# Turning the first group's rows beside two units of a bridge instead of one, in a two-layer diffusion backbone on one Trainium2 core

## The chip, the cores and the metric

The kernel runs on one core of one Trainium2 chip. The metric is the time of one execution on the device in microseconds (us); lower is better. A core has five engines that run their own instruction streams and meet at semaphores: PE (TensorE, matmuls and transposes), DVE (VectorE), ACT (ScalarE), POOL (GpSimd) and SP (SyncE, here only a queue that issues DMAs).

## The reference, cut to what matters

Two post-norm layers work on 512 latent tokens of 1024 channels and, in the first layer, on 256 context tokens beside them. Each layer is a token mixer (grouped-query attention, neighbourhood attention and Fourier mixing, merged by gates) followed by a SwiGLU channel mixer. The change touches the place where the mixer ends and the channel mixer begins:

```
y = _merge(gz, oa, ob, oc, w_branch, w_out)          # ends with  y @ w_out
x = _layernorm(DEEPNORM_ALPHA * x + g1 * y, ln1_g[l], ln1_b[l])
f = _swiglu(_modulate(_layernorm(x), sh2, sc2), w_gu[l], w_down[l])
```

So between two products (with `w_out` and with `w_gu`) there are two layer norms over the channels of a token, and a modulation by per-channel scale and shift.

## The kernel before, in words

Weights stream from memory in units of 1024 columns of 128 rows (512 KB), in two halves. SP loads a unit into `raw` (two slots), ACT copies it to `w_hi` (L797), POOL makes the remainder `w_lo` (L719), and PE takes three products per tile of the contraction (`w_lo` by `x_hi`, `w_hi` by `x_lo`, `w_hi` by `x_hi`; L2320 for a group of columns), so that fp32 accuracy comes out of a faster format. A unit of these stages is 8 steps k of 3 matmuls, 24 in all. SP may load unit u only when POOL has finished unit u-2, and ACT splits unit u+2 when PE has finished unit u.

Activations lie with channels on partitions (`acc`, `h_hi`, `h_lo`: 8 tiles of 128 channels by up to 768 tokens), but a layer norm needs tokens on partitions. A phase called `bridge` does the change-over. There are two per layer: the first, `part` 0, which the code calls `lead`, stands between `w_out` and the gate and up products; the second, `part` 1, between the down product and the next layer. A bridge splits the tokens into two groups so that the norm of one group runs beside the products of the other. For the first bridge the groups are 3 and 3 tiles of 128 tokens in layer 0 (384 columns) and 2 and 2 in layer 1 (256 columns).

PE's order in a first bridge, for group g and unit n:

1. 8 units of the first group with `w_out`; then 8 units of the second group with the same weights. After the second group's unit 0, `turn_rows` transposes the first group's `acc` to tokens on partitions (L2376).
2. `turn_columns` (L2361) transposes the normed rows `xn` back, one channel tile k at a time: it waits for `xn` of all tiles of the group at k = 0, and for `h_lo` of channel tile k-4 from k = 4 on (four PSUM banks in turn). It is called through `between`, a function that `group_columns` calls after the three matmuls of each step k. Before the change all eight calls lie in the second group's unit 7, one after each step.
3. The first gate unit of the first group (the "lead unit" below), whose step k waits for `h_lo` of channel tile k; then `turn_rows` of the second group, and so on.

ACT's order beside it, in `norm_work(0, n)` after each unit n of the second group: ACT first waits for unit n, splits unit n+2 and evacuates unit n to `acc` (L1242, `produced`), and then does a part of the norm: squares at n = 0, 2 and 3 in layer 0, `applied` at n = 5, which writes the first and, of three tiles, the third tile of `xn` (L854; DVE writes the other, L1561), and at n = 6 the DMAs that store `xr` (L867) and `modulated` for all eight channel tiles. `modulated` waits for the turned tile k, applies scale and shift in PSUM (L878), and for odd k copies it to `h_hi` (L884). DVE makes `h_hi` for even k (L1575) and `h_lo` for every k (L1569, `parts_of_h`).

Of the kernel before, what the change touches and what calls it, by code (L numbers as in the profile page):

```python
# [16 lines left out]
KD = D // P  # L17
# [159 lines left out]
def late_chunks(ph):  # L177

    return LATE if ph.kind == "bridge" and ph.layer == 0 and ph.part == 1 else 0
# [44 lines left out]
def slot_of(ph, g, i):  # L224

    return 3 * g + i if len(ph.groups[0]) < 4 else ph.groups[g][i]
# [22 lines left out]
def ends(ph):  # L249

    return ph.layer == DEPTH - 1 and ph.part == 1
# [61 lines left out]
def build(nc, x_in, ctx_in, cond, cond_cols, w_first, w_ada, b_ada, stream, qk_gain, norm_rows, bias, ident_in,  # L313
# [177 lines left out]
    def S(name):  # L491
        if name not in sems:
            sems[name] = nc.alloc_semaphore(name)
        return sems[name]
# [14 lines left out]
    def at(ph, name):  # L509

        return ph.at.get(name, 0) + (PRIME if name in PRIMED else 0)
# [60 lines left out]
    with block:  # L572
# [208 lines left out]
        def _(act):  # L781
# [54 lines left out]
            def squares(ph, g, second, some=slice(None)):  # L836

                tiles, of = ph.groups[g], xn_first if ph.kind == "first_norm" else xn
                base = (2 - ends(ph)) * len(ph.groups[0]) * g + second * len(tiles) * (ph.kind == "bridge")
                for i, t in list(enumerate(tiles))[some]:  # L840

                    act.wait_ge(S("mean_ready"), at(ph, "mean_ready") + base + i + 1)
                    if second and ph.kind == "bridge":
                        act.wait_ge(S("shifted"), at(ph, "shifted") + len(ph.groups[0]) * g + i + 1)
                    nc.scalar.activation(of[:, slot_of(ph, g, i), :], row_tile(ph, g, i, second), ACT.Square, bias=neg_mean[:, second, t:t + 1],
                                         accum_out=square_s[:, second, t:t + 1]).then_inc(S("squared"), 1)

            def applied(ph, g):

                tiles, of = ph.groups[g], xn_first if ph.kind == "first_norm" else xn  # L850
                act.wait_ge(S("root_ready"), at(ph, "root_ready") + (2 * g + 2 if ph.kind == "bridge" else 1))
                for i in range(0, len(tiles), 2):
                    t = tiles[i]
                    nc.scalar.activation(of[:, slot_of(ph, g, i), :], xr[:, t, :], ACT.Identity,  # L854
                                         scale=inv_s[:, ALLT + t:ALLT + t + 1],
                                         bias=shift_s[:, t:t + 1]).then_inc(S("normed"), 1)

            def store(ph, g):
                for i, t in enumerate(ph.groups[g]):
                    act.wait_ge(S("shifted"), at(ph, "shifted") + len(ph.groups[0]) * g + i + 1)  # L860
                    dst = out[t, :, :] if ends(ph) else scratch[2 * ph.layer + ph.part + 1, t, :, :]
                    if last_rows(ph, g) and i == len(ph.groups[g]) - 1:
                        act.dma_start(out[t, :, 0:LAT], xr[:, t, 0:LAT]).then_inc(S("stored"), 16)
                        act.wait_ge(S("shifted"), at(ph, "shifted") + len(ph.groups[0]) * g + i + 2)
                        act.dma_start(out[t, :, LAT:D], xr[:, t, LAT:D]).then_inc(S("stored"), 16)
                        continue
                    act.dma_start(dst, xr[:, t, :]).then_inc(S("stored"), 16)  # L867

            def modulated(ph, g, k):

                layer, part, m = modulated_into(ph)
                a, b = columns_of(ph.groups[g])
                if k == 0:
                    act.wait_ge(S("mods_ready"), MODS_READY[layer, part])
                act.wait_ge(S("turned"), at(ph, "turned") + KD * g + k + 1)
                for x, y, c in by_condition(a, b):
                    some = turned_columns(ph, k, x - a, y - a)
                    last = nc.scalar.activation(some, some, ACT.Identity,  # L878
                                                scale=mods_v[:, layer, m + 1, k, c:c + 1],
                                                bias=mods_v[:, layer, m, k, c:c + 1])  # L880
                last.then_inc(S("h_val"), 1)
                if k % 2:
                    act.wait_ge(S("h_val"), at(ph, "h_val") + KD * g + k + 1)
                    nc.scalar.activation(h_hi[:, k, a:b], turned_columns(ph, k, 0, b - a), ACT.Copy).then_inc(S("h_hi_odd"), 1)  # L884
# [349 lines left out]
            def bridge(ph):  # L1234
# [37 lines left out]
                def norm_work(g, n):  # L1272

                    tiles = len(ph.groups[g])
                    steps = {4: ((4, 0, 1), (5, 1, 2), (6, 2, 4)), 3: ((2, 0, 1), (3, 1, 3)),
                             2: ((3, 0, 1), (4, 1, 2)) if g and lead else ((3, 0, 2),)}[tiles]
                    if n == 0:
                        squares(ph, g, 0)
                    for step, first, end in steps:
                        if n == step:  # L1280
                            squares(ph, g, 1, slice(first, end))
                    if n == (6 if tiles > 3 else 5):
                        applied(ph, g)
                    if n == 6:
                        store(ph, g)
                        for j in range(KD):
                            modulated(ph, g, j)

                if lead:
# [974 lines left out]
        def _(pe):  # L2264
# [86 lines left out]
            def turn_columns(ph, g):  # L2351

                def between(k):
                    if k == 0:
                        even = len(ph.groups[0]) - len(ph.groups[0]) // 2
                        pe.wait_ge(S("normed"), at(ph, "normed") + even * g + (len(ph.groups[g]) + 1) // 2)
                        pe.wait_ge(S("normed_odd"), at(ph, "normed_odd") + len(ph.groups[0]) // 2 * g + len(ph.groups[g]) // 2)
                    if k >= 4:
                        pe.wait_ge(S("h_lo"), at(ph, "h_lo") + KD * g + k - 3)
                    for i in range(len(ph.groups[g])):  # L2360
                        last = nc.tensor.transpose(ps[:, TURNED_BANK[k % 4], i * P:(i + 1) * P],  # L2361
                                                   xn[:, slot_of(ph, g, i), k * P:(k + 1) * P], ident[:, :])
                    last.then_inc(S("turned"), 1)
                return between
# [431 lines left out]
            def bridge(ph):  # L2796
# [28 lines left out]
                def produced(g, n, between=lambda k: None):  # L2825

                    a, b = columns_of(ph.groups[g])
                    m = pass_unit(ph, g, n)
                    emptied(m)
                    group_columns(ph.unit + m, n % 2, m % PRODUCT_BANKS, x_hi, x_lo, k_tiles, a, b,  # L2830
                                  late_ready if g and late_chunks(ph) else ready, between
                                  ).then_inc(S("unit_done"), 1)
# [10 lines left out]
                turn = turn_columns(ph, 0)  # L2843
                for n in range(KD):
                    between = lambda k: None
                    if late_chunks(ph):
                        if n - 1 in LATE_TURNS:
                            between = lambda k: turn(LATE_TURNS[n - 1][k // 3]) if k % 3 == 1 and k // 3 < len(LATE_TURNS[n - 1]) else None
                    elif n == KD - 1 and not ends(ph):
                        between = turn  # L2850
                    produced(1, n, between)
                    if n == 0 and not late_chunks(ph):
                        turn_rows(ph, 0)
# [14 lines left out]
                for g, tiles in enumerate(ph.groups):  # L2868
                    a, b = columns_of(tiles)
                    for c in range(LEAD):  # L2870
                        u, n = first + 2 * LEAD * g + 2 * c, LEAD * g + c
# [10 lines left out]
                        else:  # L2882
                            pe.wait_ge(S("silu"), at(ph, "silu") + n)
                        group_columns(u + 1, 1, lead_bank(g, 2 * c + 1), h_hi, h_lo, KD, a, b,
                                      between=turn_columns(ph, 1) if g == 0 and c == LEAD - 1 else lambda k: None
# [68 lines left out]
            for ph in phases:  # L2954
                work = {"first_norm": first_norm, "modulate": modulate, "fourier_in": fourier_in, "tokens_a": tokens_a,
                        "fourier": fourier, "merge_c": merge_c, "merge_a": merge_a, "merge_b": merge_b, "values": values,
                        "attention": attention, "bridge": bridge, "gate_up": gate_up, "down": down}.get(ph.kind)
                if work:
                    work(ph)
# [350 lines left out]
```

## Time and profile before

| | |
|---|---|
| median of 3 runs | 2280.64 us (2278.1 to 2283.69) |
| profiled execution, its own time | 2281.39 us |
| its span in the trace | 2279.5 us |
| PE matmul busy | 2225.3 us (98%) |
| DVE, ACT, POOL busy | 1251.2, 970.6, 1140.8 us |
| mean granted TensorE clock | 0.996 |
| layer 0's first bridge | about 716 to 863 us of the span |
| layer 1's first bridge | about 1841 to 1955 us |

The span counts from the first to the last instruction of the trace; the own time adds what lies around it, 1.9 us. A timeline row gives start, duration, engine, line, operation and tiles; in square brackets stands the idle time of the engine before it and who ended it. PE rows overlap, since matmuls are pipelined: the distance of two starts tells the cost, not the duration of one.

### The profile page before, as it was taken

Reading aid. Unit: us, or ns where it says so; the run is one execution under the profiler, and the core shown is the slowest. Engines: PE = TensorE matmul, PEld = TensorE weight load, DVE = VectorE, ACT = ScalarE, POOL = GpSimd, SP = SyncE. Lnnn points to the kernel's source line nnn. Section 1 sums busy time; section 2 is a strip of 40 time slices with the busy share of each in tenths; the row PEclk is TensorE's granted clock in tenths of the full one; section 3 lists DMA queues with packets and bytes.
Section 4 is the critical chain, followed back from the end, with each engine's and each line's share of the span. In section 5 each row is a group of like instructions: output and inputs, shape, how many; then the busy total and the mean of one; then the engine's idle time right before and its main releaser. Section 6 shows DMA issues by size and latency. Waiting matters only on the chain.

```text
span 2279.5 us, 34252 instructions
## 1 busy us (share of the span) xinstructions
PE 2225.3 (98%) x12866; PEld 2034.6 (89%) x12866; DVE 1251.2 (55%) x2515; ACT 970.6 (43%) x1918; POOL 1140.8 (50%) x898
## 2 busy tenths in 40 slices
PE   7999999999999999999999999999999999999997
PEld 4899989999999999999998888888889899888887
DVE  5979766538732555875351456866548535412114
ACT  4232366537632652133232363366447456222223
POOL 1333445435634554456464653555545577544545
PEclk9999999999999999999999999999999999999999
DMA  6534300122214546412224463511223265533335
GB/s 272 213 119 130 105 26 29 47 86 75 73 56 134 169 136 208 153 61 77 78 87 138 144 225 134 194 48 37 86 83 97 85 197 185 203 94 105 110 118 184
DMA packets 122973, 273.50 MB, mean 120 GB/s; under 512 B 14020, under 2 KB 14276, under 8 KB 121032
## 3 DMA queue, kind: packets, MB, share of 16 engines
q1 hardware_dynamic: 112464, 245.42, 33.1%
q10 hardware_dynamic: 10360, 26.09, 3.4%
q8 instruction: 93, 1.52, 0.3%
q14 instruction: 56, 0.46, 0.1%
HBM read 257.82 MB, written 10.49 MB: 118 GB/s over the span
## 4 chain that ended last, share of the span: by engine, by line
PE 84%; DVE 7%; ACT 4%; DMA 2%; POOL 2%; issue 1%; ACTq 1%; SPq 0%; DVEq 0%
PE ps L2308 29%; PE ps L2320 13%; PE ps L2310 9%; PE ps L2737 8%; PE ps L2421 7%; PE ps L2915 6%; PE ps L2690 3%; PE ps L2672 3%; PE ps L2653 3%; DMA raw<-in_stream 1%; PE ps L2497 1%; POOL w_lo L719 1%; DVE pt L1911 1%; DVE max_c L1894 1%; ACT p_sb L1109 1%
## 5 line engine op out<-in xcount | busy, mean ns | idle before, releaser
L719 POOL TENSOR_TENSOR w_lo<-raw,w_hi 128x512 fp32r<-128x512 f32 x608 | 825.4, 1379 | 805.2 <-ACT w_hi L797 799.4
L797 ACT ACTIVATE w_hi<-raw 128x512 fp32r<-128x512 f32 x600 | 349.7, 627 | 567.6 <-PE ps L2308 173.5
L731 POOL TENSOR_TENSOR p_sb<-p_sb,row_inv 128x768 f32<-128x768 f32 (+1 forms) x160 | 178.9, 1126 | 195.8 <-DVE row_inv L1904 194.4
L2308 PE MATMUL ps<-h_hi,w_lo 128*128 128x512 f32 (+1 forms) x672 | 251.2, 374 | 1.1 <-POOL w_lo L719 1.1
L2308 PE MATMUL ps<-h_lo,w_hi 128*128 128x512 f32 (+1 forms) x672 | 250.5, 373 | 0.0
L2308 PE MATMUL ps<-h_hi,w_hi 128*128 128x512 f32 (+1 forms) x672 | 250.5, 373 | 0.0
L2021 DVE TENSOR_TENSOR ps<-silu_g,ps 128x512 f32<-128x512 f32 (+3 forms) x52 | 36.7, 706 | 248.4 <-PE ps L2308 172.7
L2737 PE MATMUL ps<-h_hi,w_lo 128*128 128x384 f32 (+1 forms) x408 | 146.8, 360 | 0.7 <-ACT gates_a L1146 0.7
L2737 PE MATMUL ps<-h_lo,w_hi 128*128 128x384 f32 (+1 forms) x408 | 144.2, 353 | 0.0
L2737 PE MATMUL ps<-h_hi,w_hi 128*128 128x384 f32 (+1 forms) x408 | 144.0, 353 | 0.0
L2308 PEld LDWEIGHTS ps<-h_hi,w_lo 128*128 128x128 f32 x672 | 126.2, 188 | 19.8 <-POOL w_lo L719 1.5
L2308 PEld LDWEIGHTS ps<-h_hi,w_hi 128*128 128x128 f32 x672 | 126.2, 188 | 18.3
L2308 PEld LDWEIGHTS ps<-h_lo,w_hi 128*128 128x128 f32 x672 | 126.2, 188 | 18.2
L1109 ACT ACTIVATE p_sb<-ps,neg_max 128x768 f32<-128x768 f32 (+1 forms) x160 | 117.0, 731 | 49.2 <-DVE neg_max L1891 39.6
L1911 DVE TENSOR_TENSOR pt<-ps,pt 128x512 fp32r<-128x512 f32 x176 | 118.3, 688 | 22.2 <-ACT pt L1117 20.5
L1117 ACT ACTIVATE pt<-ps 128x512 fp32r<-128x512 f32 x176 | 101.7, 598 | 57.5 <-PE ps L2672 56.6
L2320 PE MATMUL ps<-h_hi,w_lo 128*128 128x256 f32 (+2 forms) x352 | 112.2, 319 | 3.2 <-POOL w_lo L719 2.2
L2320 PE MATMUL ps<-h_lo,w_hi 128*128 128x256 f32 (+2 forms) x352 | 109.6, 311 | 0.0
L2320 PE MATMUL ps<-h_hi,w_hi 128*128 128x256 f32 (+2 forms) x352 | 109.6, 311 | 0.0
L2033 DVE SCALAR_TENSOR_TENSOR acc<-ps,mods,acc 128x256 f32<-128x256 f32 (+4 forms) x64 | 33.6, 548 | 123.7 <-PE ps L2320 64.5
L2672 PE MATMUL ps<-ident,p_sb 128*128 128x128 f32 x704 | 96.7, 275 | 2.8 <-POOL p_sb L731 1.3
L2421 PE MATMUL ps<-w_lo,h_hi 128*128 128x512 f32 (+1 forms) x272 | 96.9, 356 | 0.3 <-ACT u_cols L924 0.3
(283 smaller groups left out, 5901.8 us busy)
## 6 DMA issues: line engine op xcount, KB each, us to landing
raw<-in_stream SPq DMA_DIRECT2D x648, 256.0 KB, 3.0
ada_raw_gate_up<-in_w_ada SPq DMA_DIRECT2D x30, 512.0 KB, 4.1
ada_raw_tokens_a<-in_w_ada SPq DMA_DIRECT2D x25, 512.0 KB, 5.6
ada_raw_merge_c<-in_w_ada SPq DMA_DIRECT2D x25, 512.0 KB, 4.5
bias_sb<-in_bias ACTq DMA_DIRECT2D x32, 256.0 KB, 2.8
scratch<-xr ACTq DMA_DIRECT2D x16, 512.0 KB, 5.0
xr<-scratch SPq DMA_DIRECT2D x14, 512.0 KB, 5.3
first_raw<-in_w_first SPq DMA_DIRECT2D x5, 1024.0 KB, 14.1
```

What stands on the lines that cost most here:

```text
L719: nc.gpsimd.tensor_tensor(w_lo[:, u % 2, cols], raw[:, u % 2, cols], w_hi[:, u % 2, cols].bitcast(F32), ALU.subtract).then_inc(S("lo_made" ...
L731: nc.gpsimd.tensor_tensor(p, p, row_inv[:, c:c + 1].broadcast_to([P, keys]), ALU.mult).then_inc(S("p_ready"), 1)
L797: nc.scalar.activation(w_hi[:, s, cols], raw[:, s, cols], ACT.Copy).then_inc(S("hi_made"), 1)
L1109: nc.scalar.activation(p_sb[branch][n % 2][i][:, 0:keys], region(branch, i, 0, keys), ACT.Exp, bias=neg_max[:, i:i + 1], accum_out=row_sum ...
L1911: nc.vector.tensor_tensor(pt_lo[branch][:, a:a + w], ps[:, turn_bank(ph, order), 0:w], pt_hi[branch][:, a:a + w].bitcast(F32), ALU.subtrac ...
L2308: last = nc.tensor.matmul(bank(0), tile, x[:, k, 0:split], start=start, stop=stop)
L2310: last = nc.tensor.matmul(bank(1), tile, x[:, k, HALF:TOK], start=start, stop=stop)
L2320: last = nc.tensor.matmul(ps[:, bank, 0:b - a], w[:, s, k * P:(k + 1) * P], x[:, k, a:b], start=k == 0 and name == TERMS[0], stop=k == k_t ...
L2421: last = nc.tensor.matmul(ps[:, banks[t], 0:cols], x[:, k, t * P:(t + 1) * P], w[:, s, kk * cols:(kk + 1) * cols], start=k == 0 and name = ...
L2672: last = nc.tensor.transpose(ps[:, turn_bank(ph, order), col:col + P], p_sb[branch][n % 2][i][:, a:a + P], ident[:, :])
L2737: last = nc.tensor.matmul(ps[:, bank, 0:b - a], w[:, u % 2, k * P:(k + 1) * P], x[:, k, a:b], start=r == 0, stop=r == FILL_STEPS - 1, skip ...
L2915: last = nc.tensor.matmul(ps[:, bank, 0:HALF], half_slot(w, slot)[:, k * P:(k + 1) * P], x[:, first + k, a:a + HALF], start=FACTOR_BEGINS[ ...
```

## The change

PE calls `turn` for the first group's channel tiles 0 to 3 in the second group's unit 6 and for tiles 4 to 7 in unit 7, each after an odd step k, in place of all eight in unit 7. ACT modulates tiles 0 to 3 directly after `applied`, at n = 5 and so before it waits for unit 6, and tiles 4 to 7 at n = 6. The number of instructions stays the same. The condition leaves out the second bridge of both layers (`late_chunks` in layer 0, `ends` in layer 1), so that the first bridge of either layer is changed and nothing else; `norm_work` with g = 1 keeps its order.

```
@@ ACT, norm_work(g, n)
                     if n == (6 if tiles > 3 else 5):
                         applied(ph, g)
+                        if g == 0:
+                            for j in range(KD // 2):
+                                modulated(ph, g, j)
                     if n == 6:
                         store(ph, g)
-                        for j in range(KD):
+                        for j in range(KD // 2 * (g == 0), KD):
                             modulated(ph, g, j)
@@ PE, bridge(ph)
-                    elif n == KD - 1 and not ends(ph):
-                        between = turn
+                    elif n >= KD - 2 and not ends(ph):
+                        between = lambda k, n=n: turn((n - KD + 2) * KD // 2 + k // 2) if k % 2 else None
                     produced(1, n, between)
```

## Rows read from the trace of the kernel before

**Rows 1.** The page, parts 1 and 2: busy shares, and the granted clock by slice.

```profile
PE 2225.3 (98%) x12866; PEld 2034.6 (89%) x12866; DVE 1251.2 (55%) x2515; ACT 970.6 (43%) x1918; POOL 1140.8 (50%) x898
...
PEclk9999999999999999999999999999999999999999
```

**Rows 2.** The chain that ended last, a turn in each layer: start, us, what.

```profile
781.79 0.33 PE ps L2361 x3
...
1888.05 0.22 PE ps L2361 x2
```

**Rows 3.** Timeline of PE in layer 0, units 6 and 7 and the lead unit.

```profile
776.95 0.33 PE L2320 MATMUL ps<-y_hi,w_lo 128*128 128x384 f32 x1
...
777.82 0.33 PE L2320 MATMUL ps<-y_hi,w_hi 128*128 128x384 f32 x1
...
781.11 0.33 PE L2320 MATMUL ps<-y_hi,w_lo 128*128 128x384 f32 x1
...
781.63 0.49 PE L2361 MATMUL ps<-ident,xn 128*128 128x128 f32 x3
...
787.93 0.42 PE L2320 MATMUL ps<-h_hi,w_lo 128*128 128x384 f32 x1
```

**Rows 4.** Timeline of ACT in layer 0, from unit 5's end on.

```profile
777.15 1.15 ACT L797 ACTIVATE w_hi<-raw 128x512 fp32r<-128x512 f32 x2 [2.39 <-PE ps L2320]
...
778.82 2.37 ACT L854 ACTIVATE xn<-xr,shift_s,inv_s 128x1024 f32<-128x1024 f32 x2
...
783.18 1.21 ACT L878 ACTIVATE ps<-ps,mods 128x384 f32<-128x384 f32 x2
784.41 0.49 ACT L884 ACTIVATE h_hi<-ps 128x384 fp32r<-128x384 f32 x1
```

**Rows 5.** Timeline of PE in layer 1, units 6 and 7 and the lead unit.

```profile
1879.95 0.35 PE L2320 MATMUL ps<-y_hi,w_lo 128*128 128x256 f32 x1 [0.65 <-ACT acc L1242]
...
1880.62 0.28 PE L2320 MATMUL ps<-y_hi,w_hi 128*128 128x256 f32 x1
...
1882.91 0.36 PE L2320 MATMUL ps<-y_hi,w_lo 128*128 128x256 f32 x1
...
1887.25 0.44 PE L2361 MATMUL ps<-ident,xn 128*128 128x128 f32 x2 [1.45 <-DVE h_lo L1569]
...
1889.32 0.36 PE L2320 MATMUL ps<-h_hi,w_lo 128*128 128x256 f32 x1
```

**Rows 6.** Timeline of ACT in layer 1, the same stretch.

```profile
1880.82 1.25 ACT L854 ACTIVATE xn<-xr,shift_s,inv_s 128x1024 f32<-128x1024 f32 x1
1883.09 0.63 ACT L797 ACTIVATE w_hi<-raw 128x512 fp32r<-128x512 f32 x1 [1.03 <-PE ps L2320]
1884.81 0.63 ACT L797 ACTIVATE w_hi<-raw 128x512 fp32r<-128x512 f32 x1 [1.09 <-DMA raw<-in_stream]
...
1885.74 0.99 ACT L878 ACTIVATE ps<-ps,mods 128x256 f32<-128x256 f32 x2
```

**Rows 7.** Timeline of POOL in layer 1, the same stretch.

```profile
1878.57 6.72 POOL L719 TENSOR_TENSOR w_lo<-raw,w_hi 128x512 fp32r<-128x512 f32 x5 [1.73 <-ACT w_hi L797]
1885.52 1.26 POOL L719 TENSOR_TENSOR w_lo<-raw,w_hi 128x512 fp32r<-128x512 f32 x1 [0.23 <-ACT w_hi L797]
```

**Rows 8.** Loads of `raw` between 1878 and 1898 us, issue to landing.

```profile
DMA to landing us min/median/max: 2.6/3.6/5.4
```

**Rows 9.** Windows: us, busy (count) of PE, PEld, DVE, ACT, POOL, granted clock, DMA share, GB/s.

```profile
15.00:20.00 5.00, 0.52 (x4) 0.16 (x3) 3.65 (x6) 4.92 (x10) 0.00 (x0) 1.00 1.02 408
20.00:24.00 4.00, 4.00 (x13) 1.21 (x12) 3.63 (x10) 1.55 (x4) 2.52 (x2) 0.57 1.04 413
25.00:27.30 2.30, 0.35 (x5) 0.26 (x4) 2.30 (x4) 2.30 (x4) 0.00 (x0) 0.94 0.98 403
27.30:29.20 1.90, 1.79 (x8) 1.43 (x8) 0.79 (x6) 1.26 (x3) 1.32 (x2) 0.50 1.05 420
...
1885.50:1887.50 2.00, 0.55 (x6) 0.35 (x4) 1.16 (x3) 1.97 (x6) 1.26 (x1) 1.00 0.97 322
```

## The prediction, made before the changed kernel ran

> **What bounds the kernel now.** I read the page first: PE is busy for 98% of the span at a clock whose every slice is at full speed [rows 1]. So time moves only when PE's stream of matmuls gains or loses a gap. Then I read the chain of work that ended last in both first bridges: the turns lie on it as PE work, one of three transposes costing 0.33 us in layer 0 and one of two costing 0.22 us in layer 1 [rows 2]. The timelines of PE and ACT give the clock times of units 6 and 7, the timeline of POOL and the loads tell what a later split would do to the weights, and the windows show what the granted clock did after PE had stood idle.
>
> In layer 0, unit 6 starts at 776.95, unit 7 at 781.11, so a bare unit costs 4.16 us, 0.52 a step [rows 3]. Unit 7 with its eight turns lasts to the lead unit at 787.93: 6.82 us, and the work alone is 4.16 + 8 x 0.33 = 6.80. The turns wait for practically nothing there. ACT modulates two tiles and copies one in 783.18 to about 784.8, some 1.6 us a pair [rows 4], while PE offers a pair every 2 x (0.52 + 0.33) = 1.7 us. The two just fit.
>
> In layer 1 they don't. Unit 7 runs from 1882.91 to the lead unit at 1889.32, 6.41 us [rows 5]. Its work is 24 matmuls at 0.12 (from 1879.95 to 1880.62 five steps, the first a little longer, so 2.88) + 8 x 0.22 = 4.64. So 1.77 us are waits, 1.45 of them in one gap before the turn of tile 4, for `h_lo` of tile 0 [rows 5]. Behind it stands ACT: it could not modulate tile 0 before 1885.74, since it first waited 1.03 us for unit 6 and 1.09 us for a late half of `raw` [rows 6].
>
> **The change part by part.**
>
> *Instructions.* None is added. The turns, 8 calls per bridge, keep their 0.33 and 0.22 us each on PE, ACT's and DVE's rows their durations. The sum has only waits.
>
> *The wait for `xn` in layer 0.* The turn of tile 0 needs all rows of `xn`. ACT writes its two tiles of them at n = 5 from 778.82 to 778.82 + 2.37 = 781.19 [rows 4]; nothing in the change brings that forward, since ACT is ordered behind unit 5 (its split starts at 777.15). Before, the turn came at 781.63, 0.44 us after. Now it stands after step 1 of unit 6. The last of those six matmuls starts at 777.82 [rows 3], so PE would go on at 777.82 + 0.17 = 777.99. It stands until 781.19: a stall of 3.20 us. PE works in order: the other 18 matmuls of unit 6, which have no need of `xn`, are queued behind the turn, and unit 7 behind them. From there unit 6 ends at 781.19 + 4 x 0.33 + 6 x 0.52 = 785.63, unit 7 at 785.63 + 4.16 + 4 x 0.33 = 791.11, against 787.93 before: +3.2 us. Bounds: a stall is at least 3.1 (if PE's wait ends a little into the row's modelled end), and with a restart penalty like the 0.42 instead of 0.34 us that a first matmul shows, at most 3.4.
>
> *What is late next in layer 0.* ACT is now inside `modulated` until tile 3 is turned at 785.6 and done, 785.6 + 0.25 + 0.6 + 0.5 = 787.0; only then it splits the lead unit's weights (1.15 us, which it did from unit 6's end at 781.2 before) and POOL follows (1.3 us a half, as five of them in 6.72 us in layer 1 [rows 7]): first half at about 788.9, second at 790.2. PE wants them at 791.1 and 793.2. Hidden, with 2 us to spare. If that cover were gone the cost would be what exceeds 2 us. The modulation of tiles 4 to 7 takes ACT from 788.7 to 792.0 and the lead unit's step 7 is at 794.8: hidden as well. DVE is idle but for these. Term: 0, and between 0 and 0.5.
>
> *Layer 1.* The stall comes here too: the six matmuls of steps 0 and 1 end at 1880.62 + 0.12 = 1880.74, ACT's row of `xn` at 1880.82 + 1.25 = 1882.07 [rows 5, 6]. Loss 1.33 us. Against that the 1.77 us of waits in unit 7 go: tile 0 can be modulated at about 1882.6 in place of 1885.74, ahead of the wait for unit 6 and for the late half of `raw`, and the turn of tile 4 now comes about 3.5 us after that of tile 0 plus ACT's lead. New end of unit 7: 1882.07 + 6 x 0.36 + 4 x 0.22 = 1885.11, and + 2.88 + 0.88 = 1888.87, against 1889.32: -0.45 us. Taken: -0.5 with the gap's own restart (0.44 in place of 0.38) gone. Bounds: 0, if one of the new lags below eats it, and -1.8, if the stall for `xn` were not there.
>
> *What is late next in layer 1.* ACT splits the lead unit's two halves at about 1886.3 and 1886.9 instead of 1883.09 and 1884.81. POOL, which had finished them at 1878.57 + 6.72 = 1885.29 and 1886.78 [rows 7], finishes at about 1888.3 and 1889.6. PE wants them at 1888.9 and 1890.3: covered by 0.6 us. SP's queue is behind POOL: the loads of two units later leave 3.0 and 2.8 us later, and land 2.6 to 5.4 us after issue [rows 8], so at 1891 to 1893.7 and 1892.2 to 1895. ACT asks for them after the lead unit, at 1892.4, and PE at about 1896.4. The latest landing leaves POOL's first half done in time (1893.7 + 0.6 + 1.3 = 1895.6), and delays ACT's next work, squares of the second group, due at 1895.3, by 0.4 at most. The two stores on ACT's queue move from the end of that split to about 1887.8 and now share the DMA engines with these loads; that is in the 5.4. Term: 0, at most +0.5.
>
> Sum: +3.2 - 0.5 = +2.7 us, bounds 3.1 - 1.8 = +1.3 and 3.4 + 0.5 + 0.5 = +4.4. After the bridges everything hangs on PE's order, so the shift is carried to the end. Against the profiled execution: span 2282.2, own time 2281.39 + 2.7 = 2284.1. That execution lay 0.75 us over the median of 2280.64, so the median should be 2283.3, +0.12%. A measurement of this kernel tells about 0.3%, 6.8 us, from no change; the three runs shown lie 5.6 us apart.
>
> **The clock.** PE's new gap of 3.2 us in layer 0 is longer than any in the bridges now. What rows show: in 15 to 20 us PE did 0.52 us of work, and in 20 to 24 the clock was 0.57 of full; in 25 to 27.3 it did 0.35, and in 27.3 to 29.2 the clock was 0.50, the lower level of 1.2 GHz. After the 1.45 us gap in layer 1, in which 2 us held 0.55 us of busy time, it stayed at 1.00 [rows 9]. So 1.45 us in dense work is survived, and 2 us amid the sparse work of the start is not; 3.2 us lies between dense units and is open. The price if it falls: half of the time at 1.2 GHz. The fall after 20 us covers 0.57 x 4 us, so (1 - 0.57) x 4 x 2 = 3.4 us at half speed, which costs 1.7; one twice as long costs 3.4. The Trainium skill ("TensorE: Matmul & The Clock Gate", "Why this matters for your kernels") tells to leave no long idle gaps between bursts of matmuls, lest the clock go back to half; by that rule the new gap speaks for rival 2 and its time, and without it the sum stands. The trace agrees as far as its starting stretch goes.
>
> **The rivals.**
>
> 1. *The stall is given back.* PE's gap in layer 0 is absorbed by a wait later in the same bridge, and only layer 1's gain is left: -0.5, 2280.1 us. For it: PE has small waits after the lead unit. Against it: all of them are released by engines that PE itself releases, so they shift with it. 7%.
> 2. *The clock falls* after the gap of layer 0 and PE works at half speed for 3.4 to 6.8 us: +2.7 + 1.7 to 3.4 = +4.4 to +6.1, 2285.0 to 2286.7 us. Still within 0.3%. 15%.
> 3. *Slower, on the other side.* The same fall, but lasting: PE loses half of each microsecond at the lower level, so beyond 2 x (6.8 - 2.7) = 8.2 us at half speed the sum passes 6.8. At 10 us the price is 5, the time 2288.3. For it: nothing but that no row shows how dense work recovers here; against it: both falls at the start ended within 7 us. 4%.
> 4. *The change does what its order suggests*, and is faster: layer 0's turn does not wait for `xn` because ACT has it early, and layer 1 keeps its full 1.8 us: -1.8, 2278.8. Against it stands ACT's row [rows 4], ordered behind unit 5. It is not over 0.3% either. 2%.
>
> **How the numbers follow.** The forecast has the remaining 72%. Faster by over 0.3% would want 6.8 us of gain, and the first bridges have not 2 us of waits at this place: 0.01, for a measurement that errs. Slower: rival 3, and the upper end of rival 2 with a measurement that adds a microsecond: 0.06. Same: 0.93. The range takes the bounds +1.3 to +4.4, the spread of a median of three from runs 5.6 us apart (about 1.5 to either side), and reaches to most of rival 2 above: 2280.0 to 2287.5.
>
> **What would show it.** In layer 0 PE's row of the first turn (L2361) carries an idle time of 3.2 us, released by ACT L854, in the middle of unit 6, and the lead unit starts 3.2 us later than before. In layer 1 the same row has 1.3 us, and the gap of 1.45 us for `h_lo` is gone; the lead unit starts some 0.5 us earlier relative to unit 6. ACT's split of the lead unit comes after the modulation of tile 3, and no PE row waits for POOL there. The granted clock is 1.00 in the windows after 781 us. The prediction is wrong if that clock is 0.5 for several us, if `xn` comes earlier than 781.2, or if in layer 1 the loads of `raw` come so late that ACT and then PE stand after the lead unit.

## The result, and the profile after

The changed kernel takes 2285.74 us in the median of 8 runs (2281.65 to 2287.13), the kernel before 2281.23 us in 8 runs beside it (2277.79 to 2285.17). The ratio is 1.0018 with a 95% interval of [1.001, 1.0027]: +4.1 us, or between +2.3 and +6.2. A second series of the same kernel gave 1.002 [1.0011, 1.0029]. The predicted time of 2283.3 us is 2.4 us short of it. The range of 2280.0 to 2287.5 us held it, and the change is under 0.3%, as foreseen.

The page of the changed kernel, parts 1 and 2:

```profile
PE 2226.8 (97%) x12866; PEld 2037.6 (89%) x12866; DVE 1249.6 (55%) x2515; ACT 971.3 (43%) x1918; POOL 1144.3 (50%) x898
...
PEclk9999999999999999999999999999999999999999
```

The number of instructions is that of [rows 1], and slices of 57 us are too coarse to show anything. One has to go to the two bridges. The profiled execution took 2287.03 us, span 2285.1. Absolute times differ between executions by up to 4 us before the changed code begins, so I measure distances, called stretches below: from the first group's `turn_rows` (the first row of `ident,acc`) to the lead unit's first matmul (`h_hi,w_lo`). First the kernel before, PE's timeline, `turn_rows` in layer 0 and in layer 1:

```profile
752.76 1.91 PE L2376 MATMUL ps<-ident,acc 128*128 128x128 f32 x16
...
1862.47 1.91 PE L2376 MATMUL ps<-ident,acc 128*128 128x128 f32 x16
```

The changed kernel, PE's timeline:

```profile
749.91 1.91 PE L2379 MATMUL ps<-ident,acc 128*128 128x128 f32 x16
...
778.38 0.90 PE L2364 MATMUL ps<-ident,xn 128*128 128x128 f32 x3 [3.07 <-ACT xn L854]
...
780.04 0.52 PE L2323 MATMUL ps<-y_hi,w_lo 128*128 128x384 f32 x1
780.36 0.52 PE L2323 MATMUL ps<-y_lo,w_hi 128*128 128x384 f32 x1
...
791.13 0.42 PE L2323 MATMUL ps<-h_hi,w_lo 128*128 128x384 f32 x1
...
1866.62 1.91 PE L2379 MATMUL ps<-ident,acc 128*128 128x128 f32 x16
...
1886.19 0.44 PE L2364 MATMUL ps<-ident,xn 128*128 128x128 f32 x2 [1.25 <-ACT xn L854]
...
1894.47 0.36 PE L2323 MATMUL ps<-h_hi,w_lo 128*128 128x256 f32 x1
```

In layer 0 the stretch was 787.93 - 752.76 = 35.17 us (its end is in [rows 3]) and is 791.13 - 749.91 = 41.22: +6.05. The first turn waits 3.07 us for ACT's rows of `xn`, as foreseen. But the matmuls behind it start 0.32 us apart, and not 0.17 as in the kernel before. In layer 1 it was 1889.32 - 1862.47 = 26.85 [rows 5] and is 1894.47 - 1866.62 = 27.85: +1.00, where -0.45 was foreseen. The 1.45 us wait for `h_lo` [rows 5] is gone, and one of 1.25 us for `xn` has come. The windows of the changed kernel tell the rest; columns as in [rows 9], the granted clock is the third number from the end:

```profile
774.00:778.00 4.00, 1.30 (x8) 0.98 (x6) 0.00 (x0) 3.70 (x6) 2.49 (x2) 0.94 0.40 129
778.00:782.00 4.00, 3.62 (x14) 3.53 (x15) 1.11 (x2) 1.09 (x3) 0.00 (x0) 0.50 0.24 84
782.00:786.00 4.00, 4.00 (x21) 3.87 (x19) 1.41 (x3) 1.81 (x4) 0.00 (x0) 0.71 0.00 0
786.00:790.00 4.00, 4.00 (x28) 3.90 (x28) 1.54 (x4) 3.94 (x9) 2.39 (x2) 1.00 0.64 251
...
1885.00:1887.00 2.00, 0.81 (x6) 0.81 (x7) 0.69 (x1) 1.41 (x3) 2.00 (x3) 0.95 0.57 183
1887.00:1890.00 3.00, 3.00 (x16) 3.00 (x15) 1.27 (x3) 1.37 (x4) 1.06 (x1) 0.50 0.61 187
1890.00:1893.00 3.00, 3.00 (x26) 3.00 (x26) 1.27 (x3) 2.31 (x6) 0.43 (x1) 0.96 0.26 103
```

After the gap in layer 0 the clock stood at its lower level, 1.2 GHz. Adding (1 - clock) x length over the first three windows and doubling gives 2 x (0.24 + 2.0 + 1.16) = 6.8 us at half speed, which costs 3.4 us of PE's work less what of it fell into the gap itself. In layer 1 it is 2 x (0.1 + 1.5 + 0.12) = 3.4 us. So two things are to be told apart by experiments: the gap's own length and the clock after it.

ACT's timeline of the changed kernel in layer 0, against [rows 4]:

```profile
775.96 2.36 ACT L854 ACTIVATE xn<-xr,shift_s,inv_s 128x1024 f32<-128x1024 f32 x2
779.38 0.64 ACT L878 ACTIVATE ps<-ps,mods 128x384 f32<-128x384 f32 x1 [1.05 <-PE ps L2364]
...
786.91 0.62 ACT L797 ACTIVATE w_hi<-raw 128x512 fp32r<-128x512 f32 x1
```

ACT splits the lead unit's weights at 786.91, after the modulation of tile 3, in the order that the prediction laid out. POOL's two rows behind it start at 787.61 and take 2.54 us, so the first half was ready at about 788.9, 2 us ahead of the lead unit's start, and no PE row of the stretch waits for POOL. In layer 1 POOL's first half was ready 0.6 us ahead (1893.84 against 1894.47), as the prediction had it.

### The profile page after: what moved, and what is told of

Its sections match the earlier page's. It is cut to its first block, busy times and chain, and to the rows that moved or that the text cites. A ratio compares the mean times of both kernels' runs of the same rounds, so it can differ in the third digit from the quotient of the medians.

```text
span 2285.1 us, 34252 instructions
## 1 busy us (share of the span) xinstructions
PE 2226.8 (97%) x12866; PEld 2037.6 (89%) x12866; DVE 1249.6 (55%) x2515; ACT 971.3 (43%) x1918; POOL 1144.3 (50%) x898
## 4 chain that ended last, share of the span: by engine, by line
PE 85%; DVE 7%; ACT 4%; POOL 2%; DMA 1%; issue 1%; ACTq 1%; SPq 0%; DVEq 0%
PE ps L2311 29%; PE ps L2323 14%; PE ps L2313 9%; PE ps L2740 8%; PE ps L2424 7%; PE ps L2918 6%; PE ps L2693 3%; PE ps L2675 3%; PE ps L2656 2%; PE ps L2500 1%; DMA raw<-in_stream 1%; POOL w_lo L719 1%; DVE pt L1914 1%; DVE max_c L1897 1%; ACT p_sb L1109 1%
```

## The experiments

All variants set two tables, one entry per layer: which turn stands after which step, and how many tiles ACT modulates ahead of unit 6's wait. "Before" is eight turns in unit 7 and none ahead, "changed" the turns after odd steps of units 6 and 7 and four ahead.

```
+LEAD_TURNS = (turns of layer 0, turns of layer 1)   # {(unit, step): tile}
+TURNED_AHEAD = (ahead in layer 0, ahead in layer 1)
+APPLIED_AT = (5, 5)                                 # after which unit ACT writes its rows of xn
+EXTRA = (0, 0)                                      # extra matmuls ahead of the first turn
```

The cuts of code below give what differs from the changed kernel; "before" and "changed" stand for the whole table.

The stretches below are from the one profiled execution of each run, as above; the ratio comes from the medians of some ten executions and is to the kernel before on the same chip. The profiled execution need not be a typical one: that of the run with layer 1 alone was the slowest of its eleven, those with layer 0 alone and with early rows the fastest of nine and of eleven. Where the table has "one execution", no ratio was measured.

In layer 0 the four traces with the old order there agree to 0.03 us. In layer 1 the five with the old order there (before, layer 0 only, rows early, and the two kernels with the first turn at step 3 and at step 5) give 26.33 to 26.85, mean 26.58, so that half a microsecond says little there.

| run | layer 0: first turn waits, us at half clock, stretch | layer 1: the same | ratio, interval |
|---|---|---|---|
| before | 0, 0, 35.17 | 0 (1.45 for `h_lo`), 0, 26.85 | |
| changed | 3.07, 6.8, 41.22 | 1.25, 3.4, 27.85 | 1.0018 [1.001, 1.0027] |
| changed, 2nd | 3.07, 0, 38.47 | 1.55, 3.4, 27.86 | 1.002 [1.0011, 1.0029] |
| changed, 3rd | 3.07, 3.4, 39.76 | 1.34, 0, 26.45 | one execution |
| gap filled | 0, 0, 38.49 | 0, 0, 26.32 | 1.0022 [1.0013, 1.0031] |
| gap filled, 2nd | 0, 0, 38.50 | 1.47, 0, 27.78 | 1.0011 [1.0002, 1.002] |
| layer 0 only | 3.07, 3.4, 39.90 | as before, 0, 26.79 | 1.0027 [1.0017, 1.0037] |
| layer 1 only | as before, 0, 35.20 | 1.41, 3.4, 27.83 | 1.0 [0.9991, 1.0009] |
| rows early | 0, 0, 35.40 | as before, 0, 26.57 | 1.0002 [0.9993, 1.0011] |
| first turn at step 3 | 2.03, 3.4, 38.94 | as before, 0, 26.37 | one execution |
| first turn at step 5 | 1.00, 0, 36.39 | as before, 0, 26.33 | one execution |
| late turns in layer 1 | as before, 0, 35.18 | 0, 0, 25.25 | 0.9994 [0.9985, 1.0003] |
| the same, 2nd | as before, 0, 35.20 | 0, 0, 25.31 | 0.9993 [0.9984, 1.0002] |
| rows early, late turns | 0, 0, 35.40 | 0, 0, 25.21 | 0.9999 [0.999, 1.0009] |

**The gap filled.** The changed kernel with busy matmuls in place of the idle time.

```
+EXTRA = (18, 11)
...
+    for _ in range(EXTRA[ph.layer]):          # the bank of unit 7, which starts it anew
+        nc.tensor.matmul(ps[:, (pass_unit(ph, 1, n) + 1) % PRODUCT_BANKS, 0:b - a],
+                         w_hi[:, n % 2, k * P:(k + 1) * P], x_hi[:, k, a:b], start=True, stop=True)
```

> The changed kernel with 18 extra matmuls of 384 columns (layer 0) and 11 of 256 (layer 1) on PE between step 1 of unit 6 and the first turn, into a PSUM bank that nobody reads: the gap's time stays, its idleness goes. Theory A (the gap for xn costs its length, and the idle gap also lets the clock fall): the first turn waits under 0.3 us, the clock stays at 1.00 in both bridges, the lead unit comes 3.2 us later than before in layer 0, and the time is +2.7 us on the kernel before (ratio 1.0012), so some 1.5 to 4 us under the changed kernel. Theory B (the excess over +2.7 us is weights or loads that come late, not the clock): the time stays that of the changed kernel, ratio 1.0018 to 1.0025.

PE's timeline of this kernel in layer 0, the first turn and the lead unit (`turn_rows` began at 751.27):

```profile
779.74 0.55 PE L2369 MATMUL ps<-ident,xn 128*128 128x128 f32 x3
...
789.76 0.42 PE L2328 MATMUL ps<-h_hi,w_lo 128*128 128x384 f32 x1
```

and its windows:

```profile
774.00:778.00 4.00, 4.00 (x25) 4.00 (x24) 1.22 (x3) 2.34 (x5) 2.38 (x3) 1.00 0.42 131
778.00:782.00 4.00, 4.00 (x26) 3.68 (x25) 0.90 (x2) 2.62 (x4) 0.90 (x1) 1.00 0.41 131
```

The turn waits for nothing and the clock holds 1.00. The stretch is 38.49: +3.32, the 3.07 us of the gap and some 0.2 more. In layer 1 it is 26.32, between the -0.45 foreseen and no change, as far as the spread there tells. So the excess of the changed kernel, 2.7 us in layer 0 and 1.5 in layer 1, is not there once PE has work in the gap: Theory A, in the trace. The time was less clear. 1.0022 is above the 1.0012 that these +2.8 us would give, so I ran it again beside the changed kernel. The expectation for the filled kernel comes first, that for the changed one second.

> The kernel with the extra matmuls in the gaps once more. Theory A: clock 1.00 at both gaps, +3.3 us in layer 0 and -0.5 in layer 1, ratio 1.0012, 3 to 4 us under the changed kernel on this chip. Theory B (the extra over +2.7 us is not the clock): the same time as the changed kernel.

> The changed kernel once more, beside the one with the filled gap on the same chip. Theory A (a fall of the clock follows the gap in every execution, 3.4 or 6.8 us long): the stretch to the lead unit of layer 0 is 39.9 or 41.2 us again, that of layer 1 27.8, and the time is +5.7 to +7.1 us, ratio 1.0025 to 1.0031. Theory C (it falls in some executions only, in layer 1 above all): a stretch of 38.4 or 26.4 us turns up, and the ratio stays near 1.0018.

On one chip the changed kernel took 2284.48 us and the filled one 2282.24, ratios 1.002 and 1.0011. The difference of 2.2 us has the sign and size of the clock's share, but the intervals overlap, and in the first series the filled kernel had the higher ratio of the two (1.0022 against 1.0018): the time alone does not settle it. In the second trace of the filled kernel layer 0 is as in the first, 38.50 us at a clock of 1.00. In layer 1 the stretch is 27.78, and not for the clock, which held 1.00 there too: ACT's rows of `xn` came late, since the second half of a unit of `raw` had kept ACT waiting 1.38 us before them, and the turn waited 1.47 us in spite of the extra matmuls:

```profile
1883.12 0.63 ACT L801 ACTIVATE w_hi<-raw 128x512 fp32r<-128x512 f32 x1 [1.38 <-DMA raw<-in_stream]
1883.66 0.46 ACT L1246 ACTIVATE acc<-ps,mods 128x256 f32<-128x256 f32 x1
1884.01 1.23 ACT L858 ACTIVATE xn<-xr,shift_s,inv_s 128x1024 f32<-128x1024 f32 x1
```

The second trace of the changed kernel brought in layer 0 what Theory C had said: the same gap of 3.07 us, and no fall of the clock. Its timeline and its windows:

```profile
778.29 0.55 PE L2364 MATMUL ps<-ident,xn 128*128 128x128 f32 x3 [3.07 <-ACT xn L854]
```

```profile
775.00:779.00 4.00, 0.93 (x7) 0.71 (x6) 0.00 (x0) 3.30 (x6) 2.41 (x2) 1.00 0.45 149
779.00:783.00 4.00, 4.00 (x29) 3.90 (x27) 2.32 (x5) 2.36 (x4) 0.00 (x0) 1.00 0.09 31
```

> The changed kernel a third time, one look, for what the clock does after the gaps. Theory A: 3.4 or 6.8 us at half clock in layer 0 and 3.4 in layer 1, stretches of 39.9 or 41.2 and of 27.8 us. Theory C: the clock stays at 1.00 in one of them.

The third trace has 3.4 us at half speed in layer 0 and none in layer 1. The stretch of layer 0 in the three traces is 41.22, 38.47 and 39.76: with the time at half clock of 6.8, 0 and 3.4 us, some 1.3 to 1.4 us for each 3.4. It is one and the same program with one and the same gap, so this shows the clock's price without any change of code. Theory A as it stood ("in every execution") fell, and Theory C holds. It also weakens one reading of the filled kernel: two traces with the clock at 1.00 do not by themselves show that the extra matmuls kept it there, when one of four without them (the fourth is layer 0 alone, below) held it as well.

**What the stretches leave out.** Some 64 to 67 us behind the start of layer 1's lead unit, at the bridge's end, PE waits once more, for POOL's `w_lo` of weights whose loads reached ACT late. In the second trace of the changed kernel:

```profile
1954.87 2.58 ACT L797 ACTIVATE w_hi<-raw 128x512 fp32r<-128x512 f32 x4 [5.31 <-DMA raw<-in_stream]
...
1956.90 0.50 PE L2311 MATMUL ps<-h_hi,w_lo 128*128 128x512 f32 x1 [2.62 <-POOL w_lo L719]
```

```profile
1954.30:1956.90 2.60, 0.00 (x1) 0.01 (x1) 2.46 (x6) 1.92 (x4) 1.32 (x2) 1.00 0.82 265
1956.90:1961.00 4.10, 4.10 (x11) 3.27 (x12) 3.64 (x5) 0.55 (x1) 4.10 (x3) 0.58 0.96 344
```

The wait is 1.07 us in the kernel before, 1.79, 2.62 and 1.05 in the three traces of the changed one, 2.53 with layer 1 alone changed, 2.73 and 0.22 in the two of the filled one, and from none to 1.06 in the other seven. Behind the two of 2.62 and 2.53 us the clock fell for 3.4 us more, behind the one of 2.73 it did not. The mean is 2.0 us in the four traces with layer 1 changed and its gap unfilled, and 0.6 in the five with the old order there. That points to the change, but no run isolates it, and the measured time of layer 1 alone shows no loss (1.0); whether the change lengthens this wait stays open.

**One layer at a time.** In layer 0 first, then in layer 1.

```
LEAD_TURNS = (changed, before); TURNED_AHEAD = (4, 0)      # layer 0 only
LEAD_TURNS = (before, changed); TURNED_AHEAD = (0, 4)      # layer 1 only
```

> Only layer 0's first bridge turns over two units, layer 1's as before. Theory A: the gap of 3.1 us in layer 0 stays, 6.8 us at half clock follow it in the profile and cost about 2.9, together +3.2 to +6.1 us, ratio 1.0014 to 1.0027. Theory B (both layers carry about the same part of the measured +4.1): +2 us, ratio 1.0009.

> Only layer 1's first bridge turns over two units. Theory A: a gap of 1.25 us for xn and none of 1.45 us for h_lo: -0.45 us when the clock stays, +1.1 us when 3.4 us run at half clock, ratio 0.9998 to 1.0005. Theory B: +2 us, ratio 1.0009.

Layer 0 alone carries the loss: 1.0027, stretch +4.73 with 3.4 us at half clock. Layer 1 alone cannot be told from nothing: its ratio is 1.0. Its stretch is 27.83, 1.25 over the mean of the old order, with 3.4 us at half clock, in an execution that took 2284.18 us where the median was 2278.61. Theory B, half of the loss in each and so 1.0009, is out for layer 0, whose lower bound is 1.0017, and lies at the edge of the interval for layer 1.

**ACT's rows of `xn` one unit earlier**, which takes the gap's cause away.

```
LEAD_TURNS = (changed, before); TURNED_AHEAD = (4, 0)
-APPLIED_AT = (5, 5)
+APPLIED_AT = (4, 5)
```

> As layer 0 only, but ACT writes its rows of xn one unit earlier, after unit 4 and not after unit 5, which their root allows (shift_s was ready at 775.7 us in the trace of before, 3.1 us before ACT took it up). Theory A (the gap is ACT's place in the order, not the norm's length): the first turn of layer 0 waits 0 to 0.2 us, the clock stays at 1.00, and the time is that of the kernel before, ratio 0.9995 to 1.0005. Rival: ACT, waiting for the root, splits unit 7's weights too late and PE stands at unit 7 instead, or the turns beside two units cost PE more than beside one; then 1 to 3 us stay, ratio 1.0005 to 1.0014.

ACT's timeline and the first turn in this kernel:

```profile
772.88 2.38 ACT L858 ACTIVATE xn<-xr,shift_s,inv_s 128x1024 f32<-128x1024 f32 x2 [0.96 <-DVE shift_s L1485]
...
775.31 0.55 PE L2369 MATMUL ps<-ident,xn 128*128 128x128 f32 x3
```

Now ACT waits 0.96 us for the root of the norm, and PE waits not at all. The stretch is 35.40, +0.23, with the turns beside two units; the ratio 1.0002. So the loss of layer 0 was ACT's place in the order and what followed, and the spread turns by themselves cost 0.2 us. The rival, a late split of unit 7's weights, didn't come.

**A ladder of gaps in layer 0**: the first turn after step 3 and after step 5 of unit 6.

```
{(6,3):0, (6,5):1, (6,7):2, (7,1):3, (7,3):4, (7,5):5, (7,6):6, (7,7):7}    ahead 3
{(6,5):0, (6,7):1, (7,1):2, (7,2):3, (7,3):4, (7,5):5, (7,6):6, (7,7):7}    ahead 2
```

> Layer 0 only, the first turn after step 3 of unit 6 and not after step 1: two steps of 0.52 us fewer in the gap. Theory A: the turn waits 2.0 us, and the stretch to the lead unit grows by 2.1 us, plus 1.7 or 3.4 us if the clock falls. Rival (the clock falls only after a gap as long as 3.1 us): +2.1 us and the clock at 1.00.

> Layer 0 only, the first turn after step 5 of unit 6. Theory A: it waits 1.0 us, the stretch to the lead unit grows by 1.1 us, and the clock stays at 1.00, as it did after the 1.45 us gap of layer 1 before. Rival (a gap of 1 us is enough, as after 1.25 us in the changed kernel's layer 1): half clock for 3.4 us and +2.8 us.

The first turn and the windows around it, for step 3 and then for step 5:

```profile
781.00 0.60 PE L2369 MATMUL ps<-ident,xn 128*128 128x128 f32 x3 [2.03 <-ACT xn L858]
```

```profile
778.90:781.00 2.10, 0.07 (x1) 0.00 (x1) 0.00 (x0) 2.05 (x2) 1.24 (x2) 1.00 0.36 124
781.00:783.00 2.00, 2.00 (x9) 2.00 (x10) 0.59 (x2) 0.64 (x1) 0.00 (x0) 0.59 0.43 132
783.00:787.00 4.00, 4.00 (x23) 3.83 (x23) 1.49 (x3) 2.22 (x4) 0.00 (x0) 0.78 0.03 10
```

```profile
778.75 0.55 PE L2369 MATMUL ps<-ident,xn 128*128 128x128 f32 x3 [1.00 <-ACT xn L858]
```

```profile
777.00:779.00 2.00, 1.00 (x7) 0.68 (x6) 0.00 (x0) 1.70 (x2) 0.91 (x1) 1.00 0.44 139
779.00:781.00 2.00, 2.00 (x15) 1.96 (x14) 0.89 (x2) 0.92 (x2) 0.00 (x0) 1.00 0.34 123
```

A gap of 2.03 us was followed by 3.4 us at half speed (2 x (0.82 + 0.88)), stretch +3.77; one of 1.00 us by none, stretch +1.22. The gap's own price is its length, and 0.2 us for the turns' place, in each of the two; what the clock adds comes on top. Each has one trace, so these two do not show how often the clock falls.

**A placement that shortens layer 1's stretch.**

```
layer 1: {(6,5):0, (6,7):1, (7,0):2, (7,1):3, (7,3):4, (7,4):5, (7,6):6, (7,7):7}    ahead 4
```

> Layer 0 as before; in layer 1 the turns of tiles 0 and 1 stand after steps 5 and 7 of unit 6, those of 2 to 7 after steps 0, 1, 3, 4, 6, 7 of unit 7, and ACT modulates tiles 0 to 3 ahead of unit 6's wait. Theory A (the move is good where xn is ready and bad where it is not): the first turn waits under 0.3 us, the 1.45 us wait for h_lo is gone, the clock stays at 1.00, and from turn_rows of the first group to the lead unit it takes 25.1 us in place of 26.85; time -1.7 us, ratio 0.9992, hardly to be told from 1. Rival: the later split of the lead unit's weights takes the wait's place, and the stretch stays above 26.5 us.

> The kernel with layer 0 as before and late turns in layer 1 once more, to tell its gain of 1.6 us in the trace from none: ratio 0.9993 and, with the run before this one, an interval that should lie under 1.0003; no gain would give 1.0000.

The stretch is 25.25 and 25.31 us in two traces against 26.33 to 26.85: 1.0 to 1.6 of the 1.77 us of waits that unit 7 held. Neither series resolves it in time: 0.9994 [0.9985, 1.0003] and 0.9993 [0.9984, 1.0002]. Both ratios are on the side that the trace gives, and their intervals lie wholly under the changed kernel's. So a gain in time is likely and not shown. The last run adds the early rows in layer 0, which has nothing to win:

```
LEAD_TURNS = (changed, the table above); TURNED_AHEAD = (4, 4); APPLIED_AT = (4, 5)
```

> Layer 0 as in the run with rows written early (turns beside two units, ACT's rows of xn after unit 4), layer 1 as in the run with late turns. Theory A: no gap over 0.3 us before a first turn, clock at 1.00 in both bridges, layer 0 +0.2 us and layer 1 -1.7 us: -1.5 us, ratio 0.9993. Rival (the turns beside two units cost by themselves): ratio 1.0005 or more.

The stretches are 35.40 and 25.21, as expected. The ratio is 0.9999 [0.999, 1.0009], and this interval excludes neither the 0.9993 of Theory A nor the 1.0005 of the rival.

## Why the prediction was right, and which term was short

- *What bounds the kernel, and that only waits are in the sum*: right in the bridges. The turns cost PE the same beside two units as beside one, to 0.2 us (35.40 against 35.17 once no wait was left).
- *The wait for `xn` in layer 0, +3.2 us*: right in place, cause and size. The row has 3.07 us, released by ACT L854, and the stretch grew by 3.32 us when the clock was kept up and by 3.30 in the one trace of the changed kernel where it stayed up by itself.
- *Layer 1, -0.45 us, from a loss of 1.33 for `xn` and a gain of 1.77 for `h_lo`*: right in the waits. The gap was 1.25 us, the wait for `h_lo` vanished, and the stretch was 26.32 (gap filled) and 26.45 (changed, 3rd), 0.26 and 0.13 under the mean of the old order and within its spread, so neither sign nor size is resolved. A third trace with the clock at 1.00 (gap filled, 2nd) had 27.78, for the late half of `raw`.
- *What is late next*: right. The splits and POOL's parts of the lead unit stayed covered in both layers, by the 2 us foreseen in layer 0 and the 0.6 in layer 1. The wait at the end of layer 1's bridge, some 65 us later, was not in the sum. It differs by up to 2.7 us between the traces, so "the shift is carried to the end" holds only to that extent.
- *The clock* is the step that was short. I gave rival 2, +4.4 to +6.1 us, 15%, and took 1.00 for the likeliest; "wrong if that clock is 0.5 for several us" was my own sign, and it came, for 6.8 us in the profiled execution. Of four profiled executions with the 3.07 us gap (three of the changed kernel, one with layer 0 alone), three fell to half speed, for 6.8, 3.4 and 3.4 us. The price was 1.3 to 1.5 us for each 3.4 us, a bit under the 1.7 I had; the first window of the changed kernel has the clock falling (0.94) before the gap ended, so part of the half speed fell on idle time. And I had dismissed layer 1, since a 1.45 us gap there was survived: in the changed kernel's layer 1 gaps of 1.25, 1.41 (layer 1 only) and 1.55 us were followed by 3.4 us at half speed, one of 1.34 was not. With 1.4 us for each 3.4, layer 0's four traces average 1.4 us and layer 1's four 1.0, so the +2.7 becomes +5.1, and +4.1 and +4.6 (1.0018 and 1.002) were measured. The term of the sum that was mis-sized is thus the clock: 0 in the forecast, 2.4 us by the traces, and 1.4 to 1.9 by the time, if the rest of the sum holds. The outcome is a mixture of the forecast case and rival 2 and lies at the latter's lower end. The measured median lies above the sum's own upper bound (+4.4 us, 2285.0); the range held it by what it had added above for the measurement's spread and for rival 2.
- *Rivals 1, 3 and 4*: none was seen. No fall of the clock behind a gap lasted over 6.8 us. Nothing gave the stall back: in the filled kernel the distance from `turn_rows` in layer 0 to that in layer 1 grew from 1109.71 to 1112.97 us, by the same 3.3.

The rule of the Trainium skill ("TensorE: Matmul & The Clock Gate", "Why this matters for your kernels"), which I had set beside rival 2, to leave no long idle gaps between bursts of matmuls, spoke rightly against this change. The traces agree for the gap of 3.07 us, in three of four executions. Those of 2.03 us and of 1.25 to 1.55 us, behind which the clock fell too, are short for what one would call long.

## What to carry to other kernels

Spreading helper work over more of the main stream moves its first piece earlier, so ask first when that piece's input is ready: here ACT's order, not the arithmetic, put it 3.2 us too late, and writing the rows one unit earlier took the whole loss away, while each step by which the first turn came later took its 0.5 us off the gap. Where the old place shows a wait behind a full pipeline (layer 1), move only so far that the input is just there. And price a new idle gap on PE with half speed after it, as a probability, even where it is only one and a half or two microseconds long.

## What the runs showed of the hardware that was not expected

Whether the granted clock falls after one and the same gap differs from execution to execution. After 3.07 us of idle time in layer 0, between dense units of 384-column matmuls, it stood at 0.50 for 6.8, 0, 3.4 and 3.4 us in four executions; after 2.03 us once for 3.4, after 1.00 us once not at all. In layer 1 the wait for `h_lo` of 1.26 to 1.69 us (five executions: the kernel before, layer 0 only, rows early, first turn at step 3 and at step 5) never took the clock down, while the wait for `xn` of 1.25 to 1.55 us did in three of four. What PE did before differs: ahead of the latter stood another idle time of 0.4 to 0.6 us, six matmuls earlier. With extra matmuls between the two a wait of 1.47 us left the clock at 1.00. That this earlier gap decides was not tried by itself and stays open. Elsewhere the length of a gap decides as little: at about 252 us thirteen of the fourteen traces have a wait of 1.44 to 1.83 us for POOL's `w_lo`, and none a fall behind it; at the end of layer 1's bridge 2.62 and 2.53 us were followed by 3.4 us at half speed, and 2.73 us, in the first trace of the filled kernel, by none:

```profile
1957.42 0.50 PE L2316 MATMUL ps<-h_hi,w_lo 128*128 128x512 f32 x1 [2.73 <-POOL w_lo L723]
```

```profile
1957.40:1961.40 4.00, 3.98 (x17) 3.29 (x18) 3.50 (x5) 0.58 (x1) 4.00 (x3) 1.00 0.91 336
```

The clock also accounts for most of the 4 us by which executions differ before any changed code runs. Between 10 and 45 us of the span it was at half speed for 3.4, 6.8 or 10.2 us, whatever the kernel (mean clock 0.95, 0.90 or 0.85), and the first `turn_rows` of layer 0 began at 749.3 to 750.1, at 749.8 to 751.8, and at 752.5 to 753.3 us.
